# Two decoder layers on one core: matmuls of cleared tiles ahead of the first data, and three loads of x issued from another engine

## The reference

```python
for i in range(DEPTH):                       # DEPTH = 2, x is 1024 x 1024, mem is 256 x 1024
    mk, mv = jnp.split(mem @ w_mem_kv[i], 2, axis=-1)
    if i % 2 == 0:
        h = x @ a_w_in[j]
        q, k, v, qm = jnp.split(h, [DIL_WIDTH, 2 * DIL_WIDTH, 3 * DIL_WIDTH], axis=-1)
        mix = dilated_attention(q, k, v)
    else:
        ...
    mo = memory_attention(qm, mk, mv)
    y = jnp.concatenate([mix, mo], axis=-1) @ w_out[i]
    x = layer_norm(DN_ALPHA * x + y, ln_mix_g[i], ln_mix_b[i])
    f = (jax.nn.silu(x @ w_gate[i]) * (x @ w_up[i])) @ w_down[i]
    x = layer_norm(DN_ALPHA * x + f, ln_ffn_g[i], ln_ffn_b[i])
```

## Time and profile before

| what | value |
|---|---|
| median of 3 runs | 2153.24 us (2153.19 to 2153.7) |
| the profiled execution | 2152.82 us, of which the span in the profile is 2151.1 us |
| TensorE busy | 2121.9 us, 99% of the span |
| VectorE, ScalarE, GpSimd busy | 64%, 45%, 60% |
| DMA, mean over the span | 63 GB/s |

### The profile page before, as it was taken

One profiled execution on the slowest core, in us unless ns is written; L12 is line 12 of the kernel. 1 busy time (PEld: TensorE's weight loads), 2 busy tenths in 40 slices (PEclk: granted clock), 3 DMA queues, 4 the chain that ended last, 5 costly groups with the idle time before them and its releaser, 6 DMA issues.

```text
span 2151.1 us, 32242 instructions
## 1 busy us (share of the span) xinstructions
PE 2121.9 (99%) x10864; PEld 1804.3 (84%) x10864; DVE 1374.5 (64%) x2456; ACT 974.2 (45%) x1803; POOL 1282.1 (60%) x860
## 2 busy tenths in 40 slices
PE   8999999999999999999999999999999999999997
PEld 7888888878888888888888899988888888888885
DVE  5655555678875555656547746786965565555567
ACT  5655555654533433443324753345443343333323
POOL 5221223264598777777772793505698777777764
PEclk9999999999999999999999999999999999999998
DMA  5221111143012221111131313101022111121211
GB/s 180 71 56 45 52 57 60 35 147 99 20 60 59 59 59 49 58 51 52 44 98 50 94 45 89 70 20 40 25 69 64 54 49 58 54 59 59 59 59 79
DMA packets 167838, 134.74 MB, mean 63 GB/s; under 512 B 12720, under 2 KB 148528, under 8 KB 167728
## 3 DMA queue, kind: packets, MB, share of 16 engines
q1 hardware_dynamic: 151664, 116.93, 18.1%
q10 hardware_dynamic: 16064, 16.35, 2.6%
HBM read 124.88 MB, written 4.19 MB: 60 GB/s over the span
## 4 chain that ended last, share of the span: by engine, by line
PE 92%; DVE 4%; POOL 1%; issue 1%; ACT 1%; DMA 1%; ACTq 0%; SPq 0%; DVEq 0%; POOLq 0%
PE ps L368 27%; PE ps L370 27%; PE ps L369 27%; PE ps L724 3%; PE ps L711 2%; PE ps L752 2%; PE ps L753 1%; PE ps L712 1%; PE ps L1165 1%; POOL Rl L1887 1%; PE ps L1073 1%; DVE V L3031 1%; DMA XR<-in_x 0%; DVE T2l L1597 0%; PE ps L762 0%
## 5 line engine op out<-in xcount | busy, mean ns | idle before, releaser
L2092 DVE TENSOR_TENSOR XR<-XR,ps 128x512 f32<-128x512 f32 x504 | 338.9, 686 | 215.1 <-PE ps L370 215.0
L325 POOL TENSOR_TENSOR Wh<-raw,zcol 128x1024 fp32r<-128x1024 f32 x63 | 119.6, 1898 | 405.4 <-PE ps L370 338.3
L1887 POOL TENSOR_TENSOR Rl<-raw,Rh 128x512 fp32r<-128x512 f32 x216 | 285.9, 1325 | 121.9 <-ACT Rh L1731 119.3
L368 PE MATMUL ps<-XTh,Wh 128*128 128x512 f32 x608 | 248.6, 409 | 0.5 <-DVE bQl L935 0.4
L370 PE MATMUL ps<-XTh,Wl 128*128 128x512 f32 x608 | 238.3, 392 | 0.0
L369 PE MATMUL ps<-XTl,Wh 128*128 128x512 f32 x608 | 237.8, 391 | 0.0
L368 PE MATMUL ps<-XTh,Rh 128*128 128x512 f32 x576 | 224.2, 389 | 0.1
L370 PE MATMUL ps<-XTh,Rl 128*128 128x512 f32 x576 | 224.1, 389 | 0.0
L369 PE MATMUL ps<-XTl,Rh 128*128 128x512 f32 x576 | 224.1, 389 | 0.0
L1731 ACT ACTIVATE Rh<-raw 128x512 fp32r<-128x512 f32 x216 | 135.8, 630 | 164.2 <-PE ps L370 145.1
L1932 POOL TENSOR_TENSOR DRl<-rows,DRh 128x512 fp32r<-128x512 f32 x108 | 140.4, 1302 | 72.7 <-ACT DRh L1802 72.7
(11 more groups left out here) (351 smaller groups left out, 5676.8 us busy)
## 6 DMA issues: line engine op xcount, KB each, us to landing
raw<-in_w_up SPq DMA_DIRECT2D x44, 512.0 KB, 3.8
raw<-in_w_gate SPq DMA_DIRECT2D x72, 256.0 KB, 2.9
rows<-in_w_down SPq DMA_DIRECT2D x36, 512.0 KB, 3.6
raw<-in_a_w_in SPq DMA_DIRECT2D x19, 512.0 KB, 3.8
raw<-in_b_w_in SPq DMA_DIRECT2D x15, 512.0 KB, 3.8
B<-in_c_bias SPq DMA_DIRECT2D x12, 512.0 KB, 3.6
raw<-in_w_mem_kv SPq DMA_DIRECT2D x8, 512.0 KB, 3.8
raw<-in_w_out SPq DMA_DIRECT2D x8, 512.0 KB, 3.8
```

Source lines behind the costliest of these rows:

```text
L325: nc.gpsimd.tensor_tensor(high, raw[:, turn, :], zcol[:, 0:1].to_broadcast([P, UNIT]), ALU.add).then_inc(high_done, 1)
L368: nc.tensor.matmul(dst, wh, xh, start=first, stop=False, skip_group_check=onto)
L1887: nc.gpsimd.tensor_tensor(Rl[(w - 1) % 4][:, :], source(w), Rh[(w - 1) % 4][:, :].bitcast(F32), ALU.subtract).then_inc(gs[L]("low"), 1)
L2092: nc.vector.tensor_tensor(x, x, bank(4 + i), ALU.add).then_inc(gf[L]("added"), 1)
```

## The change

TensorE gets 22 matmuls of the cleared pieces of PTh and PTl, as soon as they are cleared; the result goes to a PSUM bank that the next product starts afresh. ScalarE issues only x tiles 0 and 1 and unit 1; after that it runs a one-column copy, ahead of which the table load now stands. SyncE, in the place where it skips unit 1, waits for the first memory tile and then issues the three 1 MB loads of x.

```diff
     X_FROM = [0, 1, 2, 4, 6, 8]
+    WARMING = 22
...
+    def x_part(eng, i):
+        eng.dma_start(XR[:, X_FROM[i]:X_FROM[i + 1], :],
+                      a["x"][0, P * X_FROM[i]:P * X_FROM[i + 1], :].rearrange("(t p) d -> p t d", p=P)
+                      ).then_inc(sem(f"landed{i}"), 16)
...
                     if (p, j) == (0, 1):
                         load.turn += 1
+                        sp.wait_ge(sem(f"landed{X_PARTS}"), 16)
+                        for i in range(2, X_PARTS):
+                            x_part(sp, i)
                     else:
                         load(sp, 3 * p + j, src[letters(p)[j]])
...
     def _(pe):
+        pe.wait_ge(*at_("cleared", 2))
+        for n in range(WARMING):
+            nc.tensor.matmul(bank(0, P), PTh[:, 0, :], PTl[:, 0, :], start=True, stop=True)
         pe.wait_ge(sem("const_landed"), 16)
...
-        for i in range(X_PARTS):
-            if i == 2:
-                act.dma_start(raw[:, 1, :].rearrange("p (k c) -> p k c", c=P), cols(a["a_w_in"][0], 3 * DIL_W)
-                              ).then_inc(raw_landed[1], 16)
-            act.dma_start(XR[:, X_FROM[i]:X_FROM[i + 1], :],
-                          a["x"][0, P * X_FROM[i]:P * X_FROM[i + 1], :].rearrange("(t p) d -> p t d", p=P)
-                          ).then_inc(sem(f"landed{i}"), 16)
+        for i in range(2):
+            x_part(act, i)
+        act.dma_start(raw[:, 1, :].rearrange("p (k c) -> p k c", c=P), cols(a["a_w_in"][0], 3 * DIL_W)
+                      ).then_inc(raw_landed[1], 16)
+        act.wait_ge(sem("zcol_set"), 1)
+        nc.scalar.activation(warm[:, :], zcol[:, :], ACT.Copy)
```

## The result

The changed kernel takes 2161.17 us in the median of 6 runs (2159.94 to 2163.49), the kernel before, run beside it, 2153.27 (2152.83 to 2153.7): ratio 1.0037, 95% interval 1.0027 to 1.0047, so 7.9 us slower. The forecast was 2157.4 with a range up to 2159.8. The direction came out, and so did the wait that was to bring it. The size did not: the loss is nearly double the 4.2 us of the sum, and outside the range. The profiled execution took 2159.94 us with a span of 2158.2, which is 7.1 us over the span before; this is the execution taken apart here.

The account below looks back on a forecast made before the run. TensorE bounds the kernel, so the q projection's start decides: unit 1 landing late delays it 4.2 us, 2152.82 + 4.2 = 2157.0, plus 0.4 for the median gives 2157.4; range 2151.6 to 2159.8.

Parts of the forecast that it names:

- the sum: Start of q projection: unit 1 lands at 20.2, GpSimd needs 4.36 us, q starts at 24.6, not 20.37: +4.2 us.
- Bound and place: Whole kernel: TensorE bounds it, busy 99% of the span; a shift of the q projection's start shifts the whole kernel.
- The moved loads: At the start: x in 4 KB rows shares packet for packet with unit 1, which lands at 20.2, 7.8 us later.
- Unit 1's slack of 3.6 us: Before the q projection: GpSimd finishes unit 1 at 16.78, q starts at 20.37, so unit 1 may land until 16.0.
- rival C: At the moved loads: x's first packet comes late, unit 1 gets away before it; -0.5 us, 2152.7; chance 0.31.
- The clock's fall: In TensorE's pause before q: a clock drop would run 3.2 us at half rate, about 1.5 us more.
- rival B: At the q projection: unit 1 late and the clock falls in the pause; +5.7 us, 2158.9; chance 0.27.
- The 22 matmuls: At the start: they take 4.6 us, end at 5.9; if the clock is up, memory transposes gain 1.5 us.
- Nothing waits for them: At the start: the 22 matmuls run from 1.3 us, ahead of data coming at 6.8, with nothing waiting for them.
- rival D: At the start: the 22 matmuls too slow or too short to raise the clock; 2153 to 2157; 0.06 with C's loads.
- with A nothing changes: A, the likeliest: unit 1 late, clock kept, +4.2, 2157.4, chance 0.36; its wait is longer than the 22 matmuls' possible losses.
- The table load: ScalarE at the start: moves from 8.08 to 4.1; k projection could start 1.4 us sooner, but the wait hides it.

Follow-up runs that it names:

- moved_only: The changed kernel without the 22 matmuls, so only the moved loads and table load: 2159.3 us, ratio 1.0029 against the kernel before.
- late_x: Changed kernel without the 22 matmuls, SyncE waiting for x tile 1 instead of the first memory tile before the three x loads: 2152.87 us, ratio 0.9999.
- unit1_sync: Changed kernel with unit 1 issued by SyncE right ahead of the three x loads, 22 matmuls kept: 2155.07 us, ratio 1.001.
- fill: Changed kernel with a wide tile of ones and 17 matmuls of it, 512 columns wide, in the pause before the q projection: 2158.43 us, ratio 1.0027.
- ones_wide: Kernel before with 10 matmuls of a tile of ones, 512 columns wide, ahead of the data: 2153.34 us, ratio 1.0.
- warm_only: Kernel before with only the 22 matmuls of cleared tiles added, loads and table load unmoved: 2154.74 us, ratio 1.0007.
- unit1_sync_wide: Changed kernel with unit 1 issued by SyncE ahead of x, and 10 matmuls of ones, 512 wide, replacing the 22: 2152.52 us, ratio 0.9998.
- unit1_sync_0: Changed kernel with unit 1 issued by SyncE right ahead of the three x loads, and without the 22 matmuls: 2153.52 us, ratio 1.0.
- zero_11: Kernel before with 11 matmuls of cleared tiles, in place of 22, ahead of the data, nothing else: 2153.41 us, ratio 1.0.

## Why the prediction was wrong

*Bound and place*: right for the loads. All but 0.2 us of what they cost came through the start of the q projection, its clock included, and was carried to the end (`moved_only`).

*The moved loads*: right in mechanism, and the number came out partly by luck. The overlap with x does starve unit 1: `late_x` and `unit1_sync` undo it in two ways, and both bring unit 1 back to 12.1 to 12.3. The first packets of x came 3.6 us after the issue, between the two bounds of 2.7 and 3.8, nearer the second; unit 1 landed at 19.4, where the sum had 20.2, and q began 3.6 us late in place of 4.2. Unit 1's slack of 3.6 us held too: of the 7.0 us by which it was later, 3.6 came through. But the sum took 9.5 for the first packet. With the measured 9.94 and a packet for a packet it gives 18.9, and for `moved_only` 17.5, where 20.1 was measured. So the slope that rival C rests on, 0.7 us of landing for every 0.1 us of the first packet, did not hold: from the one kernel to the other the first packet came 0.3 us later and unit 1 landed 0.7 us later, not 2 us sooner. Two errors, x starting late and the sharing turning against unit 1, largely cancelled.

*The clock's fall*, priced at 1.5 us and left out of the likeliest case: it happened, and cost 1.6. With it (rival B, +5.7) the forecast of the start is near the 5.1 measured at the q projection's end. I split the chance by the length of the pause, and chose the wrong side of an uncertain term. `fill` shows it. That the slow pace of the first transposes is a low clock was my reading of their spacing alone, 0.21 us against 0.11, for the granted clock reads 1.00 there. The pace halves like that where the granted clock reads 0.50: 0.43 us for a 128x512 matmul of the q projection in the changed kernel, against 0.23 at 1.00.

*The 22 matmuls*, step "Nothing waits for them", and rival D's "with A nothing changes": this is the step that put the result outside the range, whose upper end had the clock's fall in it already. Their time was right, 4.96 us against 4.6. That they would bring the clock up was wrong, at no cost here: the 16 memory transposes took 3.65 us, where the working had 1.8. That a matmul ahead does so at all was assumed; the wide ones of `ones_wide` did (2.28 us). And that they cost nothing was wrong: alone they cost 1.8 us in the medians, and beside the moved loads 1.6 us (a loss of 7.9 us in place of 6.3). The working looked only at what the 22 do in their place, not at what they move behind them. What the traces show of it is this: in `warm_only` 1.0 us is lost at 161, behind an issue that a code packet held, and 0.3 at 57, where the packet is at most a part; in the changed kernel it is 0.4 at 161 and 0.3 at 57.

In the profiled execution the terms close: 2157.0 - 0.6 (q begins sooner than forecast) + 1.6 (clock) + 2.0 (steps behind the q projection) = 2160.0, beside 2159.94. Of the 2.0, 0.4 is the held issue.

*The table load*: it did move to 4.07, and for nothing, as forecast. That it alone would start k 1.4 us sooner was wrong: the gain needs the clock up as well, as `unit1_sync_wide` shows against `ones_wide` and `unit1_sync_0`.

What stays open: the runs of the changed kernel spread over 3.5 us, those of before over 0.9, and the profiled one is the fastest of six. The median's other 1.2 us were not profiled. That a code packet holds an issue is shown at one place in six kernels; by which part of the DMA path was not tried. How much of the stall at 57 is the packet's is open, since a transfer there took 2.7 to 2.9 us in three kernels with no packet beside it and 3.0 to 3.3 in four with one. The steps at 464 and 642 us were not traced. They are not the 22 matmuls' alone: the profiled execution of `zero_11` loses 0.4 us at the first, that of `unit1_sync_0`, which has none, 0.5 us at the second.

## What to carry to other kernels

When two queues are full at once, count packets before bytes: here a load in 512-byte rows beside one in 4 KB rows moved 84 packets in a microsecond where it moved 611 alone, and later fewer still, 46 and 24. It was not through until the other nearly was. So put the one needed first ahead on the same queue, or hold the other back until it is through. A wait on weights that leaves TensorE without a matmul can cost the clock as well: here a pause of 4.0 us cost another 1.6 us, almost half of the wait again. Two stalls in a chain can hide each other: the clock and the table load brought the k projection nothing one by one and 1.3 us together. Before adding filler instructions, look where the code packets move: the same filler cost in the medians 0.1 us at 11 instructions and 1.8 at 22.

## What the runs showed of the hardware

- In the first 250 us a packet of 16 KB on the instruction queue q8 took 0.9 to 1.5 us. They started 15.6 to 22.1 us apart in the kernel before, 13.0 to 26.1 in all the kernels. An issue of a 128 KB transfer that met one ended 0.37 to 0.39 us after it, in six kernels; it took up to 1.75 us in place of 0.50.
- Of two queues that were full together, each moved as many packets as the other, 4 KB against 512 bytes: in the kernel before from 14 to 19 us, in the changed kernel from 11 to 15 (86 and 84 in 11:12). Then, in the changed kernel, the queue with 512-byte rows fell behind, to 46 beside 93 and 24 beside 141. In `moved_only` it was behind from the start (74 beside 87 in 11:12, 15 beside 100 in 17:18).
- 22 matmuls of 128 columns, one every 0.21 us for 5 us, left the following transposes at one every 0.21 us, with zeros (3.65 us for the 16 of memory) and with ones, and so did 36 for 7.9 us with zeros (3.64 us); 10 of 512 columns, one every 0.43 us, did not (2.28 us, one every 0.11). What about them decides was not settled.
- The profile reads a granted clock of 1.00 at the start of these runs, also where the transposes come one every 0.21 us, half the later pace (0.11). Where it reads 0.50, in the changed kernel from 24 us on, matmuls of 128x512 come one every 0.43 us, against 0.23 at 1.00. At the start only the spacing tells.
